# Gate and up products of experts 2 to 15 by Strassen's algorithm, with VectorE making the sums

## The reference, cut to what matters

```python
aff = softmax(t @ w_router)
gate, idx = top_k(aff.T, cap)
xe = t[idx]
hid = silu(einsum('ecd,edf->ecf', xe, w_gate)) * einsum('ecd,edf->ecf', xe, w_up)
ye = einsum('ecf,efd->ecd', hid, w_down) * gate
out = zeros(N, D).at[idx].add(ye)
```

## Time and profile before

| | |
|---|---|
| median of 3 runs | 1682.34 us (1682.12 to 1683.62) |
| profiled execution | 1680.82 us, span 1679.0 us |
| mean granted TensorE clock | 0.997 of full speed |
| TensorE, weight loads | 98%, 85% of the span |
| VectorE, ScalarE, POOL | 30%, 24%, 30% |
| transfers | 309.83 MB, mean 185 GB/s |

### The profile page before, as it was taken

One profiled execution on the slowest core, in us unless ns is written; L12 is line 12 of the kernel. 1 busy time (PEld: TensorE's weight loads), 2 busy tenths in 40 slices (PEclk: granted clock), 3 DMA queues, 4 the chain that ended last, 5 costly groups with the idle time before them and its releaser, 6 DMA issues.

```text
span 1679.0 us, 25780 instructions
## 1 busy us (share of the span) xinstructions
PE 1650.2 (98%) x10397; PEld 1421.4 (85%) x10397; DVE 505.8 (30%) x1111; ACT 404.4 (24%) x926; POOL 506.8 (30%) x465
## 2 busy tenths in 40 slices
PE   9999999999999999999999999999999999999996
PEld 6556698866898864456999999999999999999996
DVE  5575344673313640089111110111011110111105
ACT  3335134323312434454011011110111011110115
POOL 0073132532231444442132223323233122322220
PEclk9999999999999999999999999999999999999998
DMA  9311113321111627433678779887788778787794
GB/s 303 92 54 39 38 39 84 90 78 55 38 32 51 189 73 270 126 109 132 235 246 316 238 233 296 259 295 234 246 281 291 261 235 282 243 317 237 232 322 191
DMA packets 189812, 309.83 MB, mean 185 GB/s; under 512 B 12644, under 2 KB 77972, under 8 KB 189616
## 3 DMA queue, kind: packets, MB, share of 16 engines
q1 hardware_dynamic: 171840, 283.30, 49.0%
q0 software_dynamic: 17904, 25.62, 7.6%
HBM read 275.82 MB, written 33.07 MB: 184 GB/s over the span
## 4 chain that ended last, share of the span: by engine, by line
PE 91%; DVE 5%; ACT 1%; issue 1%; DMA 1%; POOL 0%; SPq 0%; DVEq 0%; ACTq 0%; POOLq 0%
PE bank L2473 33%; PE bank L2490 16%; PE bank L2186 9%; PE bank L2213 8%; PE bank L2377 5%; PE bank L2106 3%; PE bank L2142 2%; PE bank L2234 2%; PE bank L2307 2%; PE bank L2288 2%; DVE arena L1875 1%; DVE arena L1873 1%; DVE arena L1877 1%; PE bank L2152 1%; PE bank L2150 1%; PE bank L2510 1%
## 5 line engine op out<-in xcount | busy, mean ns | idle before, releaser
L2473 PE MATMUL bank<-arena 128*128 128x164 f32 x4096 | 573.0, 303 | 0.2 <-DVE arena L1982 0.2
L2473 PEld LDWEIGHTS bank<-arena 128*128 128x128 f32 x4096 | 570.8, 190 | 0.3 <-DVE arena L1982 0.3
L2490 PE MATMUL bank<-arena 128*128 128x164 f32 x1920 | 269.6, 303 | 0.0
L2490 PEld LDWEIGHTS bank<-arena 128*128 128x128 f32 x1920 | 268.0, 190 | 0.0
L973 POOL DMA_INDIRECT residual<-arena,cur_scatter x90 | 140.7, 1564 | 180.0 <-ACT arena L1455 157.2
L1992 DVE TENSOR_TENSOR arena<-bank,arena 128x328 f32<-128x328 f32 x64 | 32.0, 500 | 527.5 <-ACT arena L1444 509.9
L2186 PE MATMUL bank<-arena 128*128 128x400 f32 (+1 forms) x560 | 158.5, 445 | 0.0
L2186 PEld LDWEIGHTS bank<-arena 128*128 128x128 f32 x560 | 106.2, 190 | 51.7
L2377 PE MATMUL bank<-arena 128*128 128x512 f32 x320 | 146.0, 599 | 0.8 <-issue 0.7
L1444 ACT ACTIVATE arena<-bank 128x328 f32<-128x328 f32 x64 | 28.4, 444 | 479.3 <-PE bank L2473 457.4
L2213 PE MATMUL bank<-arena 128*128 128x192 f32 x840 | 137.7, 325 | 0.2 <-ACT arena L1014 0.2
(11 more groups left out here) (277 smaller groups left out, 1597.6 us busy)
## 6 DMA issues: line engine op xcount, KB each, us to landing
arena<-in_w_up SPq DMA_DIRECT2D x32, 2048.0 KB, 14.0
arena<-in_w_down SPq DMA_DIRECT2D x32, 2048.0 KB
arena<-in_w_gate SPq DMA_DIRECT2D x32, 2048.0 KB, 7.9
arena<-in_w_in SPq DMA_DIRECT2D x7, 1536.0 KB, 7.4
arena<-in_x_sample SPq DMA_DIRECT2D x14, 512.0 KB, 6.3
arena<-x_features_first SPq DMA_DIRECT2D x11, 512.0 KB, 8.3
arena<-decay_rows SPq DMA_DIRECT2D x22, 256.0 KB, 4.7
arena<-state_rows SPq DMA_DIRECT2D x44, 128.0 KB, 4.3
```

The lines of the kernel that those rows point to most:

```text
L2473: last = pe.matmul(ps[2 * w + fp % 2][:, a * SLOTS:(a + 1) * SLOTS], ring[2 * (fp // 2) + w][:, k, f * P:(f + 1) * P], xeT[:, k, 0:SLOTS], ...
L2490: last = pe.matmul(result_tiles(4 + dp % 2)[:, a, 0:SLOTS], ring[4 + dp // 2][:, k, dt * P:(dt + 1) * P], hidT[:, k, :], start=k == 0, sto ...
```

## The change

Experts 1 to 14 (the 2nd to the 15th) get another form of gate and up; expert 0, expert 15 and all down products keep theirs. A 1024 x 1024 matrix is cut into four 512 x 512 quarters (input features upper and lower, output features left and right), the tokens into four quarters of 512 features x 82 tokens. For each matrix w (gate, then up) seven products of a quarter with a quarter are made, each 4 x 4 = 16 matmuls of 128 x 128 weights with 82 columns, accumulated in one bank. VectorE makes four token sums an expert (T1 to T4, 328 elements a partition), four weight sums a matrix (S1 to S4, 2048 elements a partition; S3 in place) and adds the products up; ScalarE copies A1 and takes the Silu of gate in quarters. Down takes the lower half of the hidden features first. SP reloads slot 2 + w after product E2 and slot w after A2.

```diff
@@ TensorE
+                def halved_product(e, w, x, weights, tokens):
+                    to = expert_part(w, x[0])
+                    for f in range(4):
+                        for k in range(4):
+                            last = pe.matmul(to[:, f, :], weights[:, k, f * P:(f + 1) * P], tokens[:, k, :], start=f + k == 0 and x[1:] != "2",
+                                             stop=k == 3, skip_group_check=True)
+                    last.then_inc(products, 1)
+                def halved_products(e, w):
+                    a11, a12, a21, a22 = expert_weights(w)
+                    s1, s2, s4 = (expert_sum(3 * w + n) for n in range(3))
+                    t1, t2, t3, t4 = token_sums
+                    if w == 0:
+                        pe.wait_ge(rows_turned, e)
+                    pe.wait_ge(slot_in[w], e * 16 + 16)
+                    halved_product(e, w, "A1", a11, xeT[:, UPPER, ONE])
+                    pe.wait_ge(sums_made, sum_count(e, f"S2_{w}"))
+                    halved_product(e, w, "B", s2, t2)
+                    pe.wait_ge(sums_made, sum_count(e, f"S3_{w}"))
+                    halved_product(e, w, "E1", a21, t3)
+                    halved_product(e, w, "F1", s1, t1)
+                    pe.wait_ge(combined, combo_count(e, f"E{w}"))
+                    halved_product(e, w, "E2", a22, t4)
+                    pe.wait_ge(combined, combo_count(e, f"C22_{w}"))
+                    pe.wait_ge(sums_made, sum_count(e, f"S4_{w}"))
+                    halved_product(e, w, "F2", s4, xeT[:, LOWER, TWO_])
+                    pe.wait_ge(activated, activated_count(e, f"A{w}"))
+                    halved_product(e, w, "A2", a12, xeT[:, LOWER, ONE])
...
                 def down(e, dp, whole=False):
...
+                    order = tuple(range(KT)) if whole else (4, 5, 6, 7, 0, 1, 2, 3)
...
+                            if dp == 0 and a == 0 and k == 0 and not whole:
+                                pe.wait_ge(combined, combo_count(e, "hid11"))
...
+                for m in range(4):
+                    down(0, m, True)
                 with pe.Fori(0, NE - 2) as i:
+                    for w in range(2):
+                        halved_products(i + 1, w)
                     for m in range(4):
-                        down(i, m)
-                    for m in range(4):
-                        gate_up(i + 1, m)
+                        down(i + 1, m)
@@ VectorE
+                def token_halves(e):
...
+                    dve.wait_ge(rows_turned, e)
+                    sum_of(e, "T1", t1, b12, b11, ALU.subtract)
+                    sum_of(e, "T3", t3, b22, b12, ALU.subtract)
+                    dve.wait_ge(sums_made, sum_count(e, "T1"))
+                    sum_of(e, "T2", t2, b22, t1, ALU.subtract)
+                    dve.wait_ge(sums_made, sum_count(e, "T2"))
+                    sum_of(e, "T4", t4, b21, t2, ALU.subtract)
+                def weight_sum_one(e, w):
...
+                    for s in (2 + w, w):
+                        dve.wait_ge(slot_in[s], e * 16 + 16)
+                    sum_of(e, f"S1_{w}", expert_sum(3 * w), a21, a22, ALU.add)
...
+                def add_part(e, w, x, to, first, second):
+                    dve.wait_ge(products, product_count(e, w, x))
+                    dve.tensor_tensor(to, first, second, ALU.add).then_inc(combined, 1)
...
+                def halved_expert(e):
+                    weight_sum_four(e, 0)
+                    weight_sum_one(e, 1)
+                    shared(e, 0)
+                    with_e(e, 0, gates)
+                    weight_sum_two(e, 1)
+                    lower_two(e, 0, gates)
+                    lower_one(e, 0, gates)
+                    weight_sum_three(e, 1)
+                    upper_two(e, 0, gates)
+                    weight_sum_four(e, 1)
+                    shared(e, 1)
+                    with_e(e, 1, hidT)
+                    lower_two(e, 1, hidT)
+                    gated_half(e, "C22", LOWER, TWO_, "C22_1")
+                    lower_one(e, 1, hidT)
+                    gated_half(e, "C21", LOWER, ONE, "C21_1")
+                    upper_two(e, 1, hidT)
+                    gated_half(e, "C12", UPPER, TWO_, "C12_1")
+                    dve.wait_ge(activated, activated_count(e, "C11"))
+                    dve.wait_ge(products, product_count(e, 1, "A2"))
+                    dve.tensor_tensor(hidT[:, UPPER, ONE], expert_part(1, "A"), gates[:, UPPER, ONE], ALU.mult).then_inc(combined, 1)
+                def results_and_next(e, more=True):
+                    turn_rows(e + 1)
+                    if more:
+                        token_halves(e + 1)
+                    turn_results(e, 0)
+                    if more:
+                        weight_sum_one(e + 1, 0)
+                        weight_sum_two(e + 1, 0)
+                    turn_results(e, 1)
+                    if more:
+                        weight_sum_three(e + 1, 0)
+                    turn_results(e, 2)
+                    turn_results(e, 3)
@@ ScalarE
+                def halved_gates(e):
+                    act.wait_ge(products, product_count(e, 0, "A1"))
+                    act.activation(shared_part[0], expert_part(0, "A"), ACT.Copy).then_inc(activated, 1)
+                    for x, rows, cols_ in (("C22", LOWER, TWO_), ("C21", LOWER, ONE), ("C12", UPPER, TWO_)):
+                        act.wait_ge(combined, combo_count(e, x + "_0"))
+                        act.activation(gates[:, rows, cols_], gates[:, rows, cols_], ACT.Silu).then_inc(activated, 1)
+                    act.wait_ge(products, product_count(e, 0, "A2"))
+                    act.activation(gates[:, UPPER, ONE], expert_part(0, "A"), ACT.Silu).then_inc(activated, 1)
+                    act.wait_ge(products, product_count(e, 1, "A1"))
+                    act.activation(shared_part[1], expert_part(1, "A"), ACT.Copy).then_inc(activated, 1)
@@ SP
+                for s in (0, 2, 1, 3, 4, 5):
+                    if s < 4:
+                        sp.wait_ge(gu_full, 4 if s > 1 else 2)
+                    else:
+                        sp.wait_ge(dn_full, 2 * (s - 3))
+                    sp.dma_start(ring[s], expert_source(s, slice(1, 2))).then_inc(slot_in[s], 16)
+                with sp.Fori(0, NE - 2) as i:
+                    for w in range(2):
+                        sp.wait_ge(products, product_count(i + 1, w, "E2"))
+                        reload(2 + w, i + 2)
+                        sp.wait_ge(products, product_count(i + 1, w, "A2"))
+                        reload(w, i + 2)
+                    for s in (4, 5):
+                        sp.wait_ge(dn_full, i * 4 + 4 + 2 * (s - 3))
+                        reload(s, i + 2)
@@ merged semaphores
-                dve.wait_ge(gb_in, 64)
+                dve.wait_ge(vectors_in, 96)
-                        pool.wait_ge(g2_in, 16)
+                            pool.wait_ge(router_in, 48)
-                        dve.wait_ge(carry_in, 128)
+                        dve.wait_ge(carry_moved, 160)
-                dve.wait_ge(wr_in, 16)
-                dve.wait_ge(g2c_in, 16)
+                dve.wait_ge(router_in, 48)
-                pe.wait_ge(prow_in, 32)
+                pe.wait_ge(vectors_in, 96)
```

More of the change, by code:

```diff
@@ L677, in _, with reload @@
                 load_expert(3)
[L679 to L683, removed]
-                        sp.dma_start(ring[s], expert_source(s, bass.ds(i + 1, 1))).then_inc(slot_in[s], 16)
+                def reload(s, e):
+                    sp.sem_inc(passed, 1)
+                    sp.dma_start(ring[s], expert_source(s, bass.ds(e, 1))).then_inc(slot_in[s], 16)
+                for s in (0, 2, 1, 3, 4, 5):
[13 more added lines that the diff above has]
+                        reload(s, i + 2)
                 sp.dma_start(fgb, final_g.rearrange("(a n) -> a n", a=1).to_broadcast([P, D])).then_inc(fg_in, 16)
@@ L1464, in root_mean @@
                     act.activation(small[:, 16 + i:17 + i], small[:, i:i + 1], ACT.Sqrt, scale=1.0 / D, bias=small[:, 94:95]).then_inc(fin_sq, 1)
-                with act.Fori(0, NE - 1) as i:
-                    silu(i)
-                    gate_rows_of(i)
                 for fp in range(4):
-                    silu_pair(NE - 1, fp)
+                    silu_pair(0, fp)
+                gate_rows_of(0)
+                with act.Fori(0, NE - 2) as i:
+                    halved_gates(i + 1)
+                    gate_rows_of(i + 1)
+                for fp in range(4):
+                    silu_pair(1, fp)
                     for i in FIN_AT[fp]:
@@ L2039, in _ @@
                 take_quarters()
-                with dve.Fori(0, NE - 1) as i:
-                    for m in range(4):
-                        hidden(i, m)
-                    turn_rows(i + 1)
-                    for m in range(4):
-                        turn_results(i, m)
+                for m in range(4):
+                    hidden(0, m)
+                results_and_next(0)
```

(26 more changed lines are left out.)

118 lines of the change are left out of this document (87 added, 31 removed).

## The result

| | before | changed |
|---|---|---|
| median of the runs | 1682.98 us (1682.12 to 1683.81, 4 runs) | 1885.65 us (1883.79 to 1886.68, 4 runs) |
| span of the profiled execution | 1679.0 us | 1883.9 us |
| mean granted clock | 0.997 | 0.995 |

The ratio is 1.1203, 95% interval 1.1184 to 1.1222: 12% slower, 2 us from the forecast of 1883.5. The page of the changed kernel, part 1, answers to the earlier trace rows; its instruction packets to the earlier trace rows (here over the whole span, where the kernel before has 43).

The account below looks back on a forecast made before the run. TensorE alone was taken to bound the expert stage, with passes after the change paced by weight loads at 111.6 ns. Adding 201.2 us to 1680.8 gave 1882.0, plus 1.5 to the median: 1883.5 us, range 1855 to 1915.

Parts of the forecast that it names:

- The rule of 81 ns: TensorE load and matmul pair with 128 moving columns: about 81 ns, giving +0.7 us an expert; the prediction sided with 111.6.
- VectorE is hidden: VectorE's sums and adds beside the products: 32.5 us in a period of 67.8, costed at nothing.
- The sentence on sums of twice the length: VectorE's queue: even if every weight sum took twice as long, E2 and F2 would find their adds done.
- Handover: Last product to down: 0.8 us against four k steps of 1.11, covered by 0.3; uncovered, 12 us.
- ScalarE: Copies, Silus, scalings and table loads beside the products: under 10 us of 67.8, costing nothing.
- transfers: SP's six 2 MB slots, reordered: DMA share 0.65 instead of 0.82, nothing waiting behind them that is due earlier.
- merged semaphores: VectorE and POOL wait for several loads together, and the first state pass for carry stores; costs nothing.
- The few tenths at expert 0: Down's fourth pair at expert 0 waits for its bank behind S2: a few tenths of a us, once.
- The rival was real: TensorE's loop body of 1152 instructions is fetched again each round: 1898 us, at worst 1957; chance 0.05.
- the rival's price: Granted clock falls to 1.2 GHz in the products: 139.2 ns or more a pass, +26.7 us an expert, 2057 us; chance 0.03.
- The break-even: Gate and up on TensorE: at 79.5 ns a pass, 448 passes take the present 35.63 us.
- the 201.2 of the sum: Gate and up of experts 1 to 14: 50.00 us instead of 35.63, +14.37 an expert, x14 = +201.2 us.

Follow-up runs that it names:

- e1: Kernel before, with gate and up of experts 1 to 14 cut to 164, 128, 96 and 40 token columns in the four steps; 1662.7 us.
- e4: Changed kernel, with the half products over 64 of each 128 rows, half the weight bytes a load and the same 128 weight columns; 2499.4 us.
- e2: Changed kernel, with each half-product matmul cut into two of 64 weight columns, writing lower and upper 64 partitions; 1733.1 us, ratio 1.0287.
- e5: Changed kernel, with weight sums of 64 elements in place of 2048 and TensorE reading the weights themselves for S1, S2 and S4; 1885.5 us.
- e6: Changed kernel, with a reduction over 2048 elements ahead of each weight sum on VectorE, about doubling its time; 1912.5 us, ratio 1.1346.
- e9: Changed kernel, with TensorE's loop over experts written out and nothing else; 1886.4 us.
- e8: Looped changed kernel with matmuls split into two of 64 weight columns, except up's last two products, left whole; 1771.8 us, ratio 1.052.
- e11: Changed kernel, matmuls split into two of 64 weight columns, TensorE's loop written out, a quarter of each weight slot loaded for experts 2 to 15; 1639.1 us, ratio 0.9728.
- e10: Changed kernel, matmuls split into two of 64 weight columns, TensorE's loop written out, each product's last two matmuls whole; 1724.9 us, ratio 1.0237.
- e7: Changed kernel, with matmuls split into two of 64 weight columns and TensorE's loop over experts written out; 1685.4 us, ratio 1.0009.

## Why the prediction was right

- **A pass takes 111.6 ns, paced by its load.** Shown: 49.99 us for 448 passes against 50.00, e1's floor of 111 to 112 ns from 128 down to 40 columns, and e4's 112 ns with half the rows. e2 shows the converse: the same columns and products at 71.5 ns once 64 weight columns are loaded at a time; that is a little over the 65 to 70 ns that the prediction gave 82 columns. The rule of 81 ns (the Trainium skill, TensorE: Matmul & The Clock Gate, Back-to-back issue gap) is not what fp32 passes of this case do.
- **VectorE is hidden.** Shown by e5 (its sums gone, no change). Its weight sums were over-counted: 2.25 to 2.29 us each against 2.42, and with them the whole, 91.41 us in three experts (970 to 1173.4 us), 30.5 each against 32.5. The sentence on sums of twice the length was true of E2 and F2, which it named, but it left out the turns that free down's banks; e6 found 1.4 us an expert there, and 7 once at expert 0, which is the wait of 0.2 us of the changed kernel grown long.
- **Handover, ScalarE, transfers, merged semaphores.** L2680 and L2723 are idle 0.0 us before; the DMA share is 0.64 to 0.67 in windows of the stage where 0.65 was forecast. The few tenths at expert 0 are the 0.2 us behind L2082. The prediction gave POOL no price; its gathers got longer (e5) and were still in time. The price of an uncovered handover, 0.8 x 14, is 11 us and not 12.
- **The loop body is kept.** Shown by the 45 packets and by e9. The rival was real, with its place further up: 1920 instructions and more are fetched again (e8, e2).
- **The clock stayed at 1.00 in the stage.** But e1 and e4, with fewer columns or rows at the same pace, lost it, so 0.03 may have been too little, and the rival's price was too low: it let the load stay at 108 ns at the half clock, while e4 shows 212 ns a pass, which would be 448 x 0.212 = 95 us an expert.
- **The break-even.** The prediction put it at 79.5 ns a pass. e11 is on the other side of it, at 71.5, and faster than the kernel before (part of its transfers left out).
- **The last 2 us are partly luck.** The spans lie 204.9 us apart, 3.7 more than the 201.2 of the sum; 3.1 of them are the two stretches at the half clock in other stages, which the prediction didn't count. Against that stand 1.5 us that it added between the profiled execution and the median, where this kernel has none (1885.72 and 1885.65).

## What to carry to other kernels

Count weight loads as well as columns before splitting a product: in fp32 a pass with 128 weight columns takes 111.6 ns at the least, about as long as 130 token columns do (139.2 x 130 / 164 = 110, an estimate), so fewer save nothing and each further product is paid in full; Strassen's 7/8 of the columns came with 7/4 of the loads. Where columns are few, two matmuls on halves of the array load side by side, but then count instructions: their code has to arrive as well, and came late while the weights' transfers kept the DMA engines 0.83 busy.

## What the runs showed of the hardware that was not expected

- The granted clock fell to 1.2 GHz while TensorE had work in flight without a break: in e1's passes of 40 columns at 111 ns, and through most of e4's products of 64 rows and 82 columns, which ran at 112 ns before it fell and at 212 ns behind. With 128 rows and 82 columns at the same pace it stayed at 2.4 GHz for the whole expert stage.
- Two groups of 64 weight columns run as a pair in 71.5 ns; changing between whole and split matmuls and back costs 0.3 us (e10).
- A loop of 1152 instructions is fetched once, one of 1920 again and again (45 and 165 packets). Written out in sequence, code at 18 ns an instruction arrives late while the DMA engines are 0.83 busy and in time when they are 0.44 busy (e7, e11).
- POOL's gathers take 1483 ns each beside VectorE's long sums of 2048 elements and 965 ns without them (after, e5).
